# Spreading eight conditioning products of a two-layer diffusion trunk over the output projection and the up projection

## The reference

```
mod = silu(c) @ ada_w[l] + ada_b[l]                # 6 x 1024 values for each of two vectors c
sh1, sc1, g1, sh2, sc2, g2 = split(mod, 6)
h = rmsnorm(x, pre_mix_g) * (1 + sc1) + sh1
x = x + g1 * rmsnorm(token_mixing(h), post_mix_g)  # ends with gates, merge, and merged @ w_out
h = rmsnorm(x, pre_ffn_g) * (1 + sc2) + sh2
up = depthwise_conv(h @ ffn_up, 3 taps)            # 2 x 2816 columns
x = x + g2 * rmsnorm((silu(up_gate) * up_val) @ ffn_down, post_ffn_g)
```

## Time and profile before

| | |
|---|---|
| runs | 2734.06 us median of 3 (2731.23 to 2736.73) |
| profiled execution | 2733.34 us, with a span of 2731.5 us |
| busy, share of the span | PE 91%, DVE 60%, POOL 48%, ACT 20% |
| up steps 1 to 10 | 349.04 us in layer 0, 349.16 us in layer 1 |
| output projection, layer 0 | 727.08 to 784.55 us from the start |
| gap2, layer 0 | 784.55 to 826.42 us |

### The profile page before, as it was taken

One profiled execution on the slowest core, in us unless ns is written; L12 is line 12 of the kernel. 1 busy time (PEld: TensorE's weight loads), 2 busy tenths in 40 slices (PEclk: granted clock), 3 DMA queues, 4 the chain that ended last, 5 costly groups with the idle time before them and its releaser, 6 DMA issues.

```text
span 2731.5 us, 44570 instructions
## 1 busy us (share of the span) xinstructions
PE 2473.2 (91%) x15092; PEld 2303.1 (84%) x15092; DVE 1636.3 (60%) x2288; ACT 536.3 (20%) x917; POOL 1303.7 (48%) x1232
## 2 busy tenths in 40 slices
PE   7897889999978999999969888899999789999996
PEld 7894449999977998899969745699999688889995
DVE  4558756444347777765473786644451677776655
ACT  1203432110022111112221144311011211111221
POOL 1458304555534544465525761165555244445552
PEclk9998989999978999999969989999999799999998
DMA  5110103333312333222212101133332133332221
GB/s 209 57 53 13 40 8 103 117 117 97 95 43 74 104 106 102 81 72 73 66 30 85 34 10 38 39 121 117 94 114 79 28 105 104 104 103 68 72 70 58
DMA packets 100479, 211.92 MB, mean 78 GB/s; under 512 B 10208, under 2 KB 17824, under 8 KB 100384
## 3 DMA queue, kind: packets, MB, share of 16 engines
q1 hardware_dynamic: 84832, 151.66, 18.9%
q10 hardware_dynamic: 15552, 59.02, 6.0%
HBM read 207.71 MB, written 2.93 MB: 77 GB/s over the span
## 4 chain that ended last, share of the span: by engine, by line
PE 68%; DVE 12%; DVEq 11%; ACT 3%; issue 3%; DMA 1%; ACTq 1%; SPq 0%
PE ps L495 37%; PE ps L838 10%; PE ps L515 6%; DVEq L1263 4%; DVE ada_part L1260 4%; PE ps L713 3%; PE ps L565 3%; DVEq L1668 2%; PE ps L528 2%; PE ps L659 1%; DVEq L1674 1%; DVEq L1529 1%; PE ps L689 1%; PE ps L702 1%; PE ps L579 1%
## 5 line engine op out<-in xcount | busy, mean ns | idle before, releaser
L435 POOL TENSOR_SCALAR w_hi<-w_raw 128x512 fp32r<-128x512 f32 x552 | 371.8, 674 | 1222.0 <-PE ps L495 296.4
L437 POOL TENSOR_TENSOR w_lo<-w_raw,w_hi 128x512 fp32r<-128x512 f32 x552 | 758.7, 1374 | 81.4 <-issue 1.2
L495 PE MATMUL ps<-h_hi,w_hi 128*128 128x322 f32 x2688 | 636.5, 319 | 0.0
L495 PE MATMUL ps<-h_lo,w_hi 128*128 128x322 f32 x2688 | 631.9, 317 | 0.0
L495 PE MATMUL ps<-h_hi,w_lo 128*128 128x322 f32 x2688 | 627.8, 315 | 0.0
L495 PEld LDWEIGHTS ps<-h_lo,w_hi 128*128 128x128 f32 x2688 | 466.9, 194 | 0.0
L495 PEld LDWEIGHTS ps<-h_hi,w_hi 128*128 128x128 f32 x2688 | 465.2, 194 | 1.3 <-issue 1.3
L495 PEld LDWEIGHTS ps<-h_hi,w_lo 128*128 128x128 f32 x2688 | 466.1, 194 | 0.0
L1260 DVE SCALAR_TENSOR_TENSOR ada_part<-ada_raw,cond,ada_part 128x384 f32<-128x384 f32 x448 | 341.5, 803 | 19.3 <-issue 3.4
L1688 DVE TENSOR_TENSOR a_lo<-act,a_hi 128x644 fp32r<-128x644 f32 x88 | 135.3, 1541 | 148.6 <-ACT a_hi L1175 147.6
L1671 DVE SCALAR_TENSOR_TENSOR up_y<-up_x,par,up_y 128x644 f32<-128x644 f32 x176 | 179.3, 1060 | 13.2 <-issue 11.3
(11 more groups left out here) (200 smaller groups left out, 3492.4 us busy)
## 6 DMA issues: line engine op xcount, KB each, us to landing
w_raw<-in_w_lin_dram SPq DMA_DIRECT2D x360, 256.0 KB, 2.6
ada_raw<-in_w_ada_dram ACTq DMA_DIRECT2D x32, 1536.0 KB, 6.7
w_raw<-in_w_merge_dram SPq DMA_DIRECT2D x144, 256.0 KB, 2.7
ada_pre<-in_w_ada_dram ACTq DMA_DIRECT2D x4, 2048.0 KB, 21.8
w_raw<-in_w_merge_dram SPq DMA_DIRECT2D x48, 128.0 KB, 2.0
pw<-in_w_pair_dram SPq DMA_DIRECT2D x8, 640.0 KB, 3.9
x<-in_x_dram SPq DMA_DIRECT2D x8, 322.0 KB, 6.0
out_y_dram<-x SPq DMA_DIRECT2D x8, 322.0 KB, 2.3
```

Source lines behind the costliest of these rows:

```text
L435: pool.tensor_scalar(w_hi[:, s, 0:n * P], raw, 1.0, 0.0, ALU.mult, ALU.add)
L437: pool.tensor_tensor(w_lo[:, s, 0:n * P], raw, w_hi[:, s, 0:n * P], ALU.subtract).then_inc(w_split[s], 1)
L495: last = pe.matmul(ps[:, 2 * s + j, 0:HALF], w, a[:, j * HALF:(j + 1) * HALF], start=(k == 0 and i == 0), stop=(k == total - 1 and i == 2))
```

## The change

The same eight late trios are made at other places. Two move into the output projection, one stands beside the first up group, and five stay in front of P3, in steps 2, 4, 6, 8 and 9. On PE:

- trio 1 is summed in front of out's single product on set 0, and trio 2 in front of that on set 3;
- trio 3 stands in front of P0 (set 0) of step 1;
- trios 4 to 8 stand in front of P3 of steps 2, 4, 6, 8 and 9. Steps 2 to 7 are a loop of three rounds of two steps each.

On DVE, trio 1 comes before the first square of out is added, trio 2 after the fifth, and trio 3 at the start of up step 0. Trios 4 to 8 stay at the start of the same step as PE's part. ACT issues each transfer earlier to match: that of trio 1 in the last merge round, that of trio 2 in out when trio 1 is summed, that of trio 3 when out's last set is full. The small tiles hx and diag of gap2 get other addresses (`hx_up`, `diag_up`, in the space of a_hi and a_lo), since ada_raw now holds a trio during gap2.

```diff
+OUT_TRIOS = 2
+UP_TRIO_STEPS = (0, 2, 4, 6, 8, 9)
...
# PE, output projection
                     begin(L, "out", s, 1)
+                    if s == 0:
+                        ada(late_trio(L, 1), s)
+                    elif s == 3:
+                        ada(late_trio(L, 2), s)
                     product(L, "out", 2, s, two_blocks(s), merged)
...
# PE, up steps
-                with pe.Fori(1, ADA_TRIOS + 1) as i:
-                    up_step(i, True)
-                for i in range(ADA_TRIOS + 1, FFC // 2):
-                    up_step(i, False)
+                up_step(1, late_trio(L, 3), 0)
+                with pe.Fori(0, 3) as r:
+                    up_step(r * 2 + 2, late_trio(L, 4) + r)
+                    up_step(r * 2 + 3)
+                up_step(8, late_trio(L, 7))
+                up_step(9, late_trio(L, 8))
+                up_step(10)
...
# ACT, merge rounds and output projection
-                with ac.Fori(0, DC - 1) as d:
+                with ac.Fori(0, DC) as d:
                     merge_step(d)
-                merge_step(DC - 1, last_step=True)
...
+                ac.wait_ge(ada_summed, late_trio(L, 1))
+                load_ada(L, ADA_TRIOS + 1)
                 for i in range(2):
                     for j in range(4):
                         full(L, "out", j, i)
...
+                        if i == 1 and j == 0:
+                            keep_ada(j, mod[:, FFC:ADA, :], 0, 2)
+                            keep_ada(j, mod[:, 2:3, :], 2, 1).then_inc(mod_ready, 1)
+                        if i == 1 and j == 3:
+                            load_ada(L, ADA_TRIOS + 2)
+                            keep_ada(j, mod[:, ADA_TRIO:2 * ADA_TRIO, :]).then_inc(mod_ready, 1)
                         square(two(sq[:, j % 2, :]), halves(j), L, SQ_OUT + 4 * i + j, False)
...
# ACT, up steps
+                up_step(0, first=True)
+                up_step(1, keep="rows", row=2 * ADA_TRIO, trio=2, ada_set=0)
+                with ac.Fori(0, 3) as r:
+                    up_step(r * 2 + 2, keep="rows", row=r * ADA_TRIO + 3 * ADA_TRIO, trio=r)
+                    up_step(r * 2 + 3)
+                up_step(8, keep="rows", row=6 * ADA_TRIO, trio=6)
+                up_step(9, keep="last")
                 up_step(FFC // 2 - 1, last=True)
...
# DVE, output projection
+                ada(late_trio(L, 1))
                 for i in range(2):
                     for j in range(4):
                         add_square(sq_sum, j % 2, L, SQ_OUT + 4 * i + j)
+                        if i == 1 and j == 0:
+                            ada(late_trio(L, 2))
...
# DVE, up steps
-                up_step(0)
-                with dv.Fori(1, ADA_TRIOS + 1) as i:
-                    up_step(i, with_ada=True)
-                for i in range(ADA_TRIOS + 1, FFC // 2 - 1):
-                    up_step(i)
+                up_step(0, trio=late_trio(L, 3))
+                up_step(1)
+                with dv.Fori(0, 3) as r:
+                    up_step(r * 2 + 2, trio=late_trio(L, 4) + r)
+                    up_step(r * 2 + 3)
+                up_step(8, trio=late_trio(L, 7))
+                up_step(9, trio=late_trio(L, 8))
                 up_step(FFC // 2 - 1, last_step=True)
```

More of the change, by code:

```diff
@@ L355, in ada_trio, with late_trio @@
             return L * 2 * ADA_TRIOS + k
+        def late_trio(L, k):
+            return L * 2 * ADA_TRIOS + (ADA_TRIOS + k)
         def pre_tiles(i):
@@ L813, in _, with up_step @@
                 first_group(L, "up", h_part, lambda k: pe.wait_ge(h_ready, L * 2 * DC + (DC + k + 1)))
-                def up_step(i, with_ada):
+                def up_step(i, trio=None, ada_set=3):
                     for j in range(4):
                         pe.wait_ge(set_empty[j], set_use(L, "up", j, 1) + i)
-                        if j == 3 and with_ada:
-                            ada(ada_trio(L, ADA_TRIOS) + i, j)
+                        if trio is not None and j == ada_set:
+                            ada(trio, j)
                         product(L, "up", i * 2, j, two_blocks(j), h_part)
-                with pe.Fori(1, ADA_TRIOS + 1) as i:
-                    up_step(i, True)
-                for i in range(ADA_TRIOS + 1, FFC // 2):
-                    up_step(i, False)
+                up_step(1, late_trio(L, 3), 0)
[5 more added lines that the diff above has]
+                up_step(10)
                 def down_chunk(pass_, chunk, nth, slot, par_, start, stop):
@@ L1129, in _, with up_step @@
                 keep_inv_rms(L, "gap2", 2, 0, L * NINV + 2)
-                next_h(L, "gap2", 1, SQ_GAP2, L * 2 + 1, L * NINV + 3)
-                def up_step(i, first=False, last=False, keep=None):
+                next_h(L, "gap2", 1, SQ_GAP2, L * 2 + 1, L * NINV + 3, hx_up)
+                def up_step(i, first=False, last=False, keep=None, row=None, trio=None, ada_set=3):
                     for j in range(4):
@@ L1142, in up_step @@
                             ac.sem_inc(w_used[(2 * j + 1) % SLOTS], 1)
[L1143 to L1151, removed]
+                        if j == ada_set and keep is not None:
+                            if keep == "rows":
+                                if isinstance(trio, int):
+                                    load_ada(L, ADA_TRIOS + trio + 1)
+                                else:
+                                    load_ada(L, ADA_TRIOS + 4, trio)
+                                rows = mod[:, row:row + ADA_TRIO, :] if isinstance(row, int) else mod[:, bass.ds(row, ADA_TRIO), :]
+                                keep_ada(j, rows).then_inc(mod_ready, 1)
+                            else:
                                 keep_ada(j, mod[:, FFC - 1:FFC, :], 0, 1)
@@ L1175, in hi_part @@
                     ac.activation(a_hi[:, n % 2, :], src, ACT.Copy).then_inc(a_part, 1)
[L1177 to L1180, removed]
-                up_step(ADA_TRIOS, keep="last")
-                for i in range(ADA_TRIOS + 1, FFC // 2 - 1):
-                    up_step(i)
+                up_step(0, first=True)
[5 more added lines that the diff above has]
+                up_step(9, keep="last")
                 up_step(FFC // 2 - 1, last=True)
@@ L1651, in _, with up_step @@
                 dv.drain()
-                def up_step(i, last_step=False, with_ada=False):
-                    if with_ada:
-                        ada(ada_trio(L, ADA_TRIOS) + i)
+                def up_step(i, last_step=False, trio=None):
+                    if trio is not None:
+                        ada(trio)
                     for q in range(2):
```

33 lines of the change are left out of this document (16 added, 17 removed).

## The result

The changed kernel takes 2704.55 us (median of 4 runs, 2702.8 to 2705.97), and the kernel before took 2734.22 in the same comparison (4 runs, 2731.23 to 2736.73): a ratio of 0.9892, 95% interval 0.9875 to 0.9909. The forecast was 2687.5 with a range of 2658 to 2711. The sign and the range hold, but the gain is 29.7 us and not 46.6. The profiled execution took 2703.79 us, with a span of 2702.0.

The account below looks back on a forecast made before the run. The prediction took a latency chain (P3, copy, q = 1, trio, P3) as the bound, not DVE time. Up steps give 26.6 us less, out 3.7 more; 22.9 and 23.0 per layer, 45.9 in all: 2687.5 us, range 2658 to 2711.

Parts of the forecast that it names:

- The plain steps: Up steps 3, 5, 7 and 10 lose their trios and take 28.64 us each, 114.6 in sum per layer.
- DVE falls behind nowhere: Up stage: DVE needs 54.5 us in a pair of steps lasting 64.1, so its lag stays within two half steps.
- The backlog rival: DVE's and ACT's backlog from trios keeps steps 3, 5, 7 and 10 at 35.45 us; time 2742; chance 0.08.
- the loop rival: PE's longer loop body stalls at its returns, 3.2 to 4.3 us each of four; time 2700 to 2705; chance 0.06.
- The even steps: Up steps 2, 4, 6 and 8 keep trio and wait before P3: 35.45 us each, 141.8 per layer, bounds 32.76 to 36.24.
- T + 24.38: Even up steps: PE starts the twelve products 24.38 us after T, the end of the previous P3.
- the long kind: Trio steps whose twelve products and P3 take 11.86 us (2.05 + 9.81), not 10.27; expected about equally often.
- Step 9: Up step 9 follows a step with a trio and takes 35.7 us, the mean of 34.90 and 36.48.
- Step 1: Up step 1 with trio 3 at P0: 28.64 + 0.4 wait + 1.24 products = 30.3 us, against 42.61.
- The output projection: Trios 1 and 2 there: 1.24 + 1.24 products, 0.45 wait, 0.78 at set 3, 3.7 us later into gap2.
- The upper end of the range: 2711 us: all steps long, clock falling in step 1 and out, longer trio; some 12 us per layer more.
- the waits vanish: Rival: DVE gets ahead in plain steps, remaining trio steps take 29.8 us; time 2630; chance 0.08.

Follow-up runs that it names:

- trio3_set2: Changed kernel with PE summing trio 3 in front of P2 of up step 1 instead of P0; 2704.02 us, ratio 0.9894.
- quiet_pool_out: Changed kernel with GpSimd's split of weight blocks left out in the output projection alone; 2697.09 us, ratio 0.9873.
- quiet_pool_up: Changed kernel with GpSimd's split left out in the up projection alone, every trio where the change put it; 2630.58 us, ratio 0.9624.
- step_early: Changed kernel with trios 4 to 8 one DVE step earlier, summed by PE before P3 of steps 2, 4, 6, 8 and 10; 2662.59 us.
- eight_up_loads: Changed kernel with all eight trios in up steps 1 to 8, made one DVE step early, next transfer issued once DVE has read the last; 2678.51 us.
- eight_quiet_pool: eight_up_loads with GpSimd's split left out in the up projection; 2628.71 us, ratio 0.9624.
- pool_hi_only: quiet_pool_up with GpSimd's one-input instruction per block (high part) put back, the low part still left out; 2631.99 us, ratio 0.9633.

## Why the prediction was right in sign and short in size

**The plain steps** came as forecast: 28.56 us each, where 28.64 was taken. The backlog rival fell with them. (That DVE falls behind nowhere, as the prediction had it, holds only just at the start of the stage: in trio3_set2, whose step 1 has no wait, DVE has no pause from trio 3 to the end of trio 4 but for the tanh, and PE waits the longer in step 2.) So did the loop rival: in step 4, which follows a return of the longer body, PE came to P3 at 990.69 - 3.10 = 987.59, that is 21.46 us after T, against 21.42 for three quarters of a plain step: no gap. The section that the prediction set against its trace, the Trainium skill's "Runtime: NRT & Kernel Launch", section "Instruction fetch mechanics", also gives PE's instruction memory as 2048 instructions. Either body (528, or 396 products with as many weight loads) fits into that, so that page and trace needn't differ.

**The even steps** had the right chain. The forecast put PE's start at T + 24.38; in step 4 it was at 990.69 - 966.13 = T + 24.56. The size was off behind it: the twelve products and P3 were taken as 11.07 us, the mean of two lengths of before, and here took 11.97 (990.69 to 1002.66). All four even steps of layer 0 were of the long kind, 35.97, 36.53, 36.51 and 36.46, in sum 145.5 against 141.8. Three of them lie a little above the upper bound named (36.24). Why none of the even steps is of the short kind any more isn't settled. Step 9, the one directly behind a step with a trio, was: it took 34.82, against 35.7.

**Step 1** was taken as 30.3 us and took 33.52. DVE began the trio 11.98 us before PE came to P0 (856.10 and 869.86 - 1.78), where the forecast had 12.36. But the trio took 13.53 us, so PE waited 1.78 and not 0.4. Then the clock fell: the products took 1.47 and the rest 30.27 us instead of 1.24 and 28.64.

**The output projection** was taken as 3.7 us more, the start of gap2 included, and cost 6.9 in layer 0 (63.53 - 57.47 and 42.70 - 41.87) and 6.3 in layer 1 (2048.95 to 2112.46, and a gap2 of 42.14). Trio 2 began where the forecast had it: 766.4 moves to 770.9 with the later start of the stage (731.57 against 727.08), and it was 770.99. It ended at 784.67 and not by 784.0, and PE waited 1.54 and not 0.45. The rest is the clock again: P3 ran its first pairs at 0.74 us.

**The step that failed** is mainly one term, in two places: the length of a trio, which the prediction took as 11.90 to 13.02 us, and, hanging on it, the clock that was to stay up behind a short wait. Both rows were read rightly, but they were rows of a DVE beside a GpSimd that split less. The windows of the trios in those rows, columns as in the earlier trace rows (the fifth time is GpSimd's):

```profile
505.23:517.13 11.90, 11.90 (x83) 11.90 (x82) 11.37 (x17) 0.80 (x1) 5.27 (x7) 1.00 0.19 55
910.74:923.76 13.02, 10.00 (x67) 9.73 (x66) 12.37 (x18) 0.71 (x1) 6.06 (x6) 1.00 0.28 81
```

and those of trio 2 and trio 3 of the changed kernel:

```profile
770.99:784.67 13.68, 12.27 (x83) 12.01 (x81) 13.16 (x17) 2.52 (x4) 8.30 (x9) 1.00 0.27 78
856.10:869.63 13.53, 11.98 (x81) 11.71 (x79) 13.01 (x16) 1.42 (x2) 6.96 (x7) 1.00 0.31 78
```

Against the 9.60 us of a trio with no split beside it, each is longer by about half of GpSimd's busy time in it (2.3 us for 5.27, 3.4 for 6.06, 4.1 for 8.30, 3.9 for 6.96). GpSimd's last split beside the trio of step 2 of before:

```profile
918.25 1.40 POOL L437 TENSOR_TENSOR w_lo<-w_raw,w_hi 128x512 fp32r<-128x512 f32 x1
```

It ended at 919.65 us, 4.1 us before the trio did: PE stood waiting for the trio and no block came free. In the output projection PE has other products to make meanwhile, and the splits go on to the trio's end. Beside trio 3 GpSimd stands still at the end too, for 2.8 us (from 866.86), so that there the row of 13.02 was off by 0.5 us only.

quiet_pool_out shows that this is the cause in the output projection: 9.98 us, no wait, and 3.47 us less in the stage. quiet_pool_up shows it for step 1: trio 3 takes 9.7 us there (845.56 to 855.24), and the wait is gone. Of the 6.4 us by which step 1, the output projection and gap2 exceed their terms in layer 0, the longer waits are 2.5, and nearly all of the rest is time at the lower clock behind them. The smaller term is the even steps' products and P3 (3.7 us per layer, of which step 9 and the plain steps give back 1.2).

The upper end of the range, 2711, had put the same signs together: the long kind everywhere, the clock falling in step 1 and in out, and the longer of the two lengths of a trio, some 12 us per layer more. About 8 came (16.4/2, below). So the range holds since it priced the fall of the clock at its edge; GpSimd's part in a trio's length stands nowhere in it. The number of PE's waits was off for the same reason: 16 and not ten to fourteen, with 37.7/16 = 2.4 us in the mean and not 3.

In sum the shortfall is 5.6 us in the up steps (328.05 against 322.4) and 3.2 in the output projection and gap2 in layer 0, 4.6 and 2.6 in layer 1: 16.0 of the 16.4 us by which the profiled execution (2703.79) misses the sum's 2687.4. The stretches between, which the change leaves alone, vary by up to 4.5 us each and cancel nearly.

The sentence that failed in the argument is "It isn't a lack of DVE time, since DVE has idle time inside it". For the changed kernel it is half true: step_early gains 42 us by order alone. For eight trios in a row it is wrong: eight_up_loads, with order and transfers cured, is bound by DVE's 30 us of work in a step of 33.25, and 8.7 us of that work (30.01 against 21.33 in eight_quiet_pool) went when GpSimd's split went. The rival "the waits vanish", 2630 us, was put down at 0.08 since the order stood against it. quiet_pool_up keeps that order and takes 2630.58: the chain is 6.65 us shorter without contention, which is twice the wait.

The Trainium skill's "SBUF — State Buffer", section "Who interferes with whom", says that a DVE instruction with two inputs in SBUF contends with a GpSimd instruction that reads SBUF, since DVE's second input comes through an interface that the two share. The runs agree: L1282 reads two such inputs and falls from 828 to 615 ns without the split. Here the cost to a trio was about 1.0 us per block of 128x512 beside it.

## What to carry to other kernels

A duration from the trace holds for the company it was measured in: before using it elsewhere, look at what the neighbouring engines did in that row's window and what they will do in the new place, above all when the row lies inside a wait that is about to vanish. When work is moved to close a wait of 1 to 3 us, a miss of 1 us on the wrong side can cost the fall of the clock as well (here 1.1 us of extra wait became 3 us). And where one engine prepares operands beside another's arithmetic, price the pair, not each alone.

## What the runs showed of the hardware beyond that

GpSimd's split lengthened not only the two-input instructions of DVE: the convolution's first multiply, with one input and a column of parameters, took 904 ns in the mean in the changed kernel (L1691, 42 instructions) and 635 in quiet_pool_up. In pool_hi_only it took 642, so nearly all of the lengthening comes with the low part, GpSimd's instruction with two inputs.

The clock's fall isn't decided by the length of a wait alone. In eight_up_loads PE waited 2.37 us for GpSimd at the same place of three steps: behind that at 966.42 the next pairs took 0.74 us, behind those at 1032.92 and 1066.15 they took 0.46 (mean granted clock of the three steps: 0.95, 1.00 and 1.00). In the changed kernel the clock was down behind waits of 1.54 and 1.78 us and the twelve one-column products that follow them, where before it had stayed up behind a wait of 1.18 us without such products.
